# First feed-forward's output projection as seven block products, its weight sums on GpSimd, and 12 modulation tiles moved behind the convolution

## The reference, cut to what matters

```
mod_x = split(silu(c) @ w_ada + b_ada, 9)          # 9 x 1024 modulation values, and mod_c from c_ctx
def ffn_half(s, shift, scale, gate, g_pre, g_post, w_in, w_out):
    h = (silu(gate_part) * up_part) @ w_out         # gate_part, up_part = split(modulate(rmsnorm(s, g_pre)) @ w_in)
    return s + 0.5 * gate * rmsnorm(h, g_post)
xs = ffn_half(xs, ...)                              # 256 tokens, D_FF = 2816, D_MODEL = 1024
cs = ffn_half(cs, ...)                              # 256 context tokens, the same weights
hx = modulate(rmsnorm(xs, g[2]), mod_x[3], mod_x[4])
hc = modulate(rmsnorm(cs, g[2]), mod_c[3], mod_c[4])
z_hy, q, k, v, gates = split(hx @ w_in)             # z_hy: 3 x 1024 columns, then a 3-tap convolution over tokens
```

## Time and profile before

| | us |
|---|---|
| median of 3 runs | 1926.42 (1924.99 to 1927.2) |
| the profiled execution's own time | 1927.17 |
| its span | 1925.4 |
| TensorE busy | 1732.5 (90%) |
| VectorE busy | 874.4 (45%) |
| ScalarE busy | 308.7 (16%) |
| GpSimd busy | 164.6 (9%) |

### The profile page before, as it was taken

The page is one execution under the profiler, slowest core; times in us unless marked ns, Lnnn a source line. Parts: engine busy times, 40 slices in busy tenths (PEclk is TensorE's granted clock), DMA queues, the critical chain, the costliest instruction groups (busy, mean ns, idle before and its releaser), DMA issues.

```text
span 1925.4 us, 28951 instructions
## 1 busy us (share of the span) xinstructions
PE 1732.5 (90%) x11848; PEld 1371.0 (71%) x11848; DVE 874.4 (45%) x1760; ACT 308.7 (16%) x697; POOL 164.6 (9%) x159
## 2 busy tenths in 40 slices
PE   8999999999999999999999999999999765655656
PEld 3888888888888989679999998877778221221214
DVE  5766666965466466644676136743433000000001
ACT  2200000010210002422111114322323000000001
POOL 3000000010133310001000002612001000000000
PEclk9999999999999999999999999989999987787878
DMA  9433334965442214126545863101379999999997
GB/s 374 148 130 129 128 130 160 346 244 197 153 153 88 88 45 154 66 87 220 195 171 179 291 213 130 45 24 46 131 279 377 407 430 433 430 432 433 430 432 302
DMA packets 47043, 426.04 MB, mean 221 GB/s; under 512 B 5364, under 2 KB 5973, under 8 KB 16093
## 3 DMA queue, kind: packets, MB, share of 16 engines
q1 hardware_dynamic: 37296, 386.97, 51.7%
q10 hardware_dynamic: 9644, 37.59, 5.4%
HBM read 423.49 MB, written 1.05 MB: 220 GB/s over the span
## 4 chain that ended last, share of the span: by engine, by line
PE 71%; DMA 18%; DVE 5%; issue 2%; ACT 2%; POOL 1%; POOLq 0%; SPq 0%; ACTq 0%; DVEq 0%
PE bank L1027 26%; DMA arena<-experts_ring_dram 18%; PE bank L1161 13%; PE bank L1211 8%; PE bank L1595 3%; PE bank L1310 3%; PE bank L1308 3%; PE bank L1664 2%; PE bank L1969 2%; PE bank L1488 1%; ACT arena L2254 1%; DVE arena L3232 1%; DVE tiny L3034 1%; PE bank L1363 1%; PE bank L1353 1%
## 5 line engine op out<-in xcount | busy, mean ns | idle before, releaser
L1027 PE MATMUL bank<-arena 128*128 128x256 f32 (+1 forms) x2912 | 507.5, 336 | 0.5 <-ACT arena L2471 0.5
L1027 PEld LDWEIGHTS bank<-arena 128*128 128x128 f32 x2912 | 459.2, 191 | 46.6 <-issue 1.8
L1969 PE MATMUL bank<-arena 128*32 128x512 f32 x1400 | 213.2, 763 | 145.3 <-DMA arena<-experts_ring_dram 145.3
L1969 PEld LDWEIGHTS bank<-arena 128*32 128x32 f32 x1400 | 58.1, 135 | 293.5 <-issue 293.3
L1161 PE MATMUL bank<-arena 128*128 128x256 f32 x880 | 193.9, 379 | 0.0
L1161 PEld LDWEIGHTS bank<-arena 128*128 128x128 f32 x880 | 167.1, 190 | 23.1 <-issue 0.5
L1211 PE MATMUL bank<-arena 128*128 128x128 f32 x1456 | 162.9, 275 | 0.0
L1211 PEld LDWEIGHTS bank<-arena 128*128 128x128 f32 x1456 | 162.8, 192 | 0.1
L3426 DVE TENSOR_TENSOR arena<-arena,bank 128x512 f32<-128x512 f32 x8 | 5.5, 688 | 240.8 <-PE bank L1969 240.8
L905 POOL TENSOR_TENSOR rstd<-sq 128x128 f32<-128x128 f32 (+2 forms) x9 | 6.7, 740 | 971.6 <-ACT sq L2091 971.6
L2732 DVE SCALAR_TENSOR_TENSOR arena<-arena 128x1024 f32<-128x1024 f32 x56 | 68.3, 1221 | 0.0
(11 more groups left out here) (500 smaller groups left out, 2233.8 us busy)
## 6 DMA issues: line engine op xcount, KB each, us to landing
arena<-dense_dram SPq DMA_DIRECT2D x167, 1024.0 KB, 4.9
arena<-experts_ring_dram SPq DMA_DIRECT2D x41, 4096.0 KB, 26.9
arena<-ada_rest_dram ACTq DMA_DIRECT2D x56, 512.0 KB, 5.5
arena<-experts_dram SPq DMA_DIRECT2D x18, 1024.0 KB, 8.8
arena<-ada_head_dram SPq DMA_DIRECT2D x8, 1024.0 KB, 23.6
arena<-experts_dram SPq DMA_DIRECT2D x10, 512.0 KB, 9.4
arena<-tokens_dram ACTq DMA_DIRECT2D x1, 2048.0 KB, 20.7
arena<-experts_ring_dram SPq DMA_DIRECT2D x1, 2048.0 KB, 23.5
```

Source lines behind the costliest of these rows:

```text
L1027: ins = mm(out, lhsT=w, rhs=rhs(k), start=k == 0, stop=k == k_tiles - 1)
L1969: ins = mm(ps[banks[half]][32 * e:32 * e + 32, :], lhsT=lhs[:, 2 * kp + par, CAP * e:CAP * e + CAP], rhs=slab[e][par][:, half * 512:half * ...
```

## The change

`ffn1_out` is computed as seven block products too. A pair of output tiles (2p, 2p+1) is one step p of 4, for r=0 and then r=1. The 22 hidden blocks split into two halves of 11, and the 11 go in three slabs c of 4, 4 and 3 blocks in each half; seven 128-column accumulation regions in two banks (0,1 for even p, 2,3 for odd p) stay open over the three slabs. That makes 24 slabs of which every third is only three quarters full, where there were 22.

- TensorE: `out_products`, 7 x 4 (or 7 x 3) matmuls of 128 columns in each slab.
- GpSimd: for each of the 24 slabs four tensor_tensors of 128 x 512 (128 x 384 for the third slab), after it has waited for all of `hid1`; `sum_squares(2)` stands behind slab 17.
- VectorE: four token sums for each c and r (24 tensor_tensors of SBUF data, 128 x 512 or 128 x 384), five joins for each (r, p) out of the banks, and 16 ada tiles instead of 28 in r=0, in groups of four ahead of the join of each p; 8 in r=1 as before, in two groups; the other 12 stand in the loop over `z`, one after each of tiles 2 to 13.
- ScalarE: one 128 x 128 copy for each (r, p), and the squares are taken from SBUF after the join. Its 8 last ada loads stand in the `z` loop.
- The context's norm (`stat_of_sum(3)`, `inverse_root(3)`) and its residual start one tile of `z` later.

```diff
-ADA_FIRST, ADA_SECOND = 28, 8
+ADA_FIRST, ADA_SECOND = 16, 8
+OUT_HALF, OUT_STEPS = FT // 2, 3
+OUT_SUMMED = KD * OUT_STEPS
@@ GpSimd
-            sum_squares(2, T)
+            pool.wait_ge(in_hid, FT)
+            for n in range(OUT_SUMMED):
+                slab, s, made, nk = SLAB0["ffn1_out"] + n, n % 2, 4 * FT + 4 * n, len(out_step(n % OUT_STEPS))
...
+                pool.wait_ge(slab_loaded[slab % RING], 16 * (slab // RING + 1))
+                if n > 1:
+                    pool.wait_ge(ws_used, FT + n - 1)
+                nc.gpsimd.tensor_tensor(s1, w2, w3, add).then_inc(ws_ready, 1)
+                pool.wait_ge(ws_ready, made + 1)
+                nc.gpsimd.tensor_tensor(s2, s1, w0, sub).then_inc(ws_ready, 1)
+                nc.gpsimd.tensor_tensor(w2, w0, w2, sub).then_inc(ws_ready, 1)
+                pool.wait_ge(ws_ready, made + 2)
+                nc.gpsimd.tensor_tensor(s4, w1, s2, sub).then_inc(ws_ready, 1)
+                if n == OUT_SUMMED // 2 + 5:
+                    sum_squares(2, T)
@@ TensorE
+            def out_products(r, p, c):
...
+                out_region(a, 0, w0, first_a, nk, first, False, slab_started)
+                out_region(a, P, w1, first_b, nk, False, False)
+                pe.wait_ge(ot_ready, 12 * r + 4 * c + 2)
+                pe.wait_ge(ws_ready, 4 * FT + 4 * n + 2)
+                out_region(a, 2 * P, s2, t2, nk, False, False)
+                ins = out_region(a, 3 * P, s1, t1, nk, False, last)
...
+                pe.wait_ge(ot_ready, 12 * r + 4 * c + 4)
+                pe.wait_ge(ws_ready, 4 * FT + 4 * n + 4)
+                out_region(b, 0, s4, second_b, nk, first, False)
+                out_region(b, P, w2, t3, nk, False, False)
+                ins = out_region(b, 2 * P, w3, t4, nk, False, last, ws_used)
...
-            for t in range(2 * KD):
-                take(pe, "ffn1_out", t % 4, t // 4)
-                product(ps[t % 4][:, 0:T], FT, lambda k: x_then_ctx(t, k), full[t % 4],
-                        arrived=None if t else last_hidden(in_hid))
-                first_norms(t)
+            for r in range(2):
+                for p in range(KD // 2):
+                    for c in range(OUT_STEPS):
+                        out_products(r, p, c)
+                        if (r, p, c) == (1, 0, 1):
+                            stat_of_sum(1, T)
+                        elif (r, p, c) == (1, 2, 1):
+                            stat_of_sum(2, T)
@@ VectorE
+            def out_token_sums(r, c):
+                a1, a2, b1, b2 = out_hidden(r, c)
+                t1, t2, t3, t4 = out_tokens(r, c)
+                tt_(t1, a2, a1, sub).then_inc(ot_ready, 1)
...
+                tt_(t2, b2, t1, sub).then_inc(ot_ready, 1)
+                tt_(t3, b2, a2, sub).then_inc(ot_ready, 1)
...
+                tt_(t4, b1, t2, sub).then_inc(ot_ready, 1)
...
+            for p in range(KD // 2):
+                for n in range(ADA_FIRST // 4 * p, ADA_FIRST // 4 * p + ADA_FIRST // 4):
+                    ada_late(n, y1[:, 0:4, T:2 * T])
+                if p:
+                    out_sums(0, p - 1)
+                out_join_first(0, p)
+                if p == KD // 2 - 1:
+                    got(dve, "ffn1_out", 3, 1)
+                    out_token_sums(1, 0)
+                out_join_second(0, p)
+            for c_ in range(1, OUT_STEPS):
+                out_token_sums(1, c_)
+            out_sums(0, KD // 2 - 1)
...
+            out_join_first(1, 0)
+            out_join_second(1, 0)
+            for p in range(2):
+                for n in range(ADA_SECOND // 2):
+                    ada_late(ADA_FIRST + ADA_SECOND // 2 * p + n, page(7, D).rearrange("p (k n) -> p k n", n=T))
+                if p == 0:
+                    out_sums(1, 0)
+                    out_join_first(1, 1)
+                    out_join_second(1, 1)
...
+            for p in range(2, 4):
+                out_sums(1, p - 1)
+                out_join_first(1, p)
+                out_join_second(1, p)
+            out_sums(1, 3)
@@ VectorE, the loop over z
-                if 1 <= n <= KD + 1:
-                    ctx_residual(n - 1)
+                if 2 <= n <= KD + 2:
+                    ctx_residual(n - 2)
...
+                if 2 <= n < 2 + ADA_TILES - ADA_IN - ADA_FIRST - ADA_SECOND:
+                    ada_late(ADA_FIRST + ADA_SECOND + n - 2, fh)
```

More of the change, by code:

```diff
@@ L253, in slabs, with out_slabs @@
     return b.reshape(-1, 16, P, P).transpose(0, 2, 1, 3).reshape(-1, P, SLAB)
+def out_slabs(w):
+    b = blocks(w)
+    out = np.zeros((KD // 2, OUT_STEPS, 16, P, P), b.dtype)
+    for p in range(KD // 2):
+        for c in range(OUT_STEPS):
+            ks = list(out_step(c))
+            for n, (o, lo) in enumerate(((0, 0), (0, OUT_HALF), (1, 0), (1, OUT_HALF))):
+                out[p, c, n * len(ks):n * len(ks) + len(ks)] = b[2 * p + o][[lo + k for k in ks]]
+    return slabs(out)
 def wide(w, n=256):
@@ L299, in lay_out @@
     dense = np.concatenate([
-        slabs(f1), *(slabs(blocks(g["w_ff_out"][0, 0])) for _ in range(2)), slabs(blocks(w_in[:, :5 * D])),
+        slabs(f1), *(out_slabs(g["w_ff_out"][0, 0]) for _ in range(2)), slabs(blocks(w_in[:, :5 * D])),
         wide(w_in[:, 5 * D:6 * D]), slabs(first_gates[:2 * GATE_PAIRS]),
@@ L623, in build @@
         in_hid = sem("in_hid")
+        ot_ready = sem("ot_ready")
         tt_ready = sem("tt_ready")
@@ L930, in _ @@
             for n in range(8):
-                slab, s, made = SLAB0["k"] + n, n % 2, 4 * FT + 4 * n
+                slab, s, made = SLAB0["k"] + n, n % 2, 4 * (FT + OUT_SUMMED) + 4 * n
                 w0, w1, w2, w3 = kv_blocks(n)
@@ L1267, in ctx_norms, with out_region @@
                     stat_of_sum(4, T)
+            def out_region(b, o, lhs, rhs, n, start, stop, started=None):
+                for k in range(n):
+                    ins = mm(ps[b][:, o:o + P], lhsT=lhs[:, k, :], rhs=rhs[:, k, :], start=start and k == 0, stop=stop and k == n - 1)
+                    if k == 0 and started is not None:
+                        ins.then_inc(started, 1)
+                return ins
+            def out_products(r, p, c):
+                n, nk, (a, b), use = 12 * r + 3 * p + c, len(out_step(c)), TWO_SETS[p % 2], 2 * r + p // 2
+                s, first, last = n % 2, c == 0, c == OUT_STEPS - 1
+                slot = st.slab % RING
+                assert st.slab == SLAB0["ffn1_out"] + n
+                w0, w1, w2, w3 = (ring[slot][:, m * nk:m * nk + nk, :] for m in range(4))
+                s1, s2, s4 = (v_[s] for v_ in (out_s1, out_s2, out_s4))
+                first_a, _, first_b, second_b = out_hidden(r, c)
+                t1, t2, t3, t4 = out_tokens(r, c)
+                pe.wait_ge(slab_loaded[slot], 16 * (st.slab // RING + 1))
+                st.slab += 1
+                if r == p == 0:
+                    pe.wait_ge(in_hid, OUT_HALF + out_step(c)[-1] + 1)
+                if first:
+                    take(pe, "ffn1_out", a, use)
+                out_region(a, 0, w0, first_a, nk, first, False, slab_started)
[4 more added lines that the diff above has]
+                ins = out_region(a, 3 * P, s1, t1, nk, False, last)
+                if last:
+                    ins.then_inc(full[a], 1)
+                if first:
+                    take(pe, "ffn1_out", b, use)
+                pe.wait_ge(ot_ready, 12 * r + 4 * c + 4)
[3 more added lines that the diff above has]
+                ins = out_region(b, 2 * P, w3, t4, nk, False, last, ws_used)
+                if last:
+                    ins.then_inc(full[b], 1)
             def last_hidden(made):
@@ L2195, in _ @@
                 square(2, j, X[:, j, 0:T], T)
[L2196 to L2203, removed]
+            for p in range(KD // 2):
+                if p == 2:
+                    root(2, T)
+                out_copy(1, p)
+                out_squares(1, p)
+                if p < 2:
+                    for n in range(ADA_SECOND // 2):
+                        ada_late_load(ADA_FIRST + ADA_SECOND // 2 * p + n)
             for n in range(24):
```

118 lines of the change are left out of this document (84 added, 34 removed).

## The result

The changed kernel takes 1962.31 us (median of 4 runs, 1960.02 to 1962.5) against 1926.14 for the kernel before in the same comparison: ratio 1.0185 [1.0168, 1.0203], slower by 36 us. The forecast was 1978 us, with a range of 1940 to 2002. The profiled execution took 1962.5 us with a span of 1960.6, so its rows explain the measured time.

The account below looks back on a forecast made before the run. The prediction took TensorE (90% of the span) as the bound before the change. It summed 1927.2 + 42 (stage) + 6 (z) + 4 (clock) = 1979, given as 1978 us against the median of the runs, range 1940 to 2002.

Parts of the forecast that it names:

- rival 2: `ffn1_out`: turns are taken but orders interlock better, port hardly rests; stage +30, z +3, clock 0: 1960 us; chance 23%.
- TensorE's gain, -16.7: `ffn1_out`: 1232 records of 128 columns take 137.9 us in place of 154.6; alone -16.7 us.
- Turns, 2.22 us each: `ffn1_out`: VectorE's ada operations and GpSimd's 512-wide sums alternate at the SBUF port, 1.27 + 1.22 - 0.27 = 2.22 us.
- The port budget as floor, 181: `ffn1_out`: GpSimd and VectorE two-SBUF-input work, less turn savings, needs at least 181 us against 154.6 before.
- The turn to r=1: Slab 12: TensorE waits from 414 to 430 us for VectorE's token sums, queued behind the join of step 3.
- The norm's wait, 440.8 to 444.7: First norm in r=1: TensorE waits 440.8 to 444.7 us behind VectorE's eight token sums and two square sums.
- The end: End of `ffn1_out`: slab 18's s2 at 470.5, TensorE done about 514, z starts at 519.3 us; stage +42.
- z, +6: z: VectorE falls 11 us behind, banks allow 10.6; waits for residual, reciprocal and squares cost +6 us (bounds 0 and 14).
- Clock, +4: `ffn1_out`: TensorE's granted clock drops after long waits, partly hidden by following waits; +4 us (bounds 0 and 20).
- Rival 1: `ffn1_out`: ada operations don't collide with GpSimd, TensorE stays the bound: 1919.6 us, faster; chance 13%.
- Rival 3: `ffn1_out` and z: 1.2 GHz clock after each long wait, +20 instead of +4, z lateness at upper bound: 2000 us; 11%.
- Rival 4: `ffn1_out`: 128-column products keep starving and miss 0.112 us, other waits just balance: within 0.2%; chance 3%.

Follow-up runs that it names:

- e2: Changed kernel with GpSimd's weight sums cut to 32 columns and TensorE multiplying the slab's own blocks in their place: 1917.23 us, ratio 0.9949.
- e1b: Changed kernel with the stage's 24 ada tiles reading their second input from a bank, in four 512-column operations a tile: 1925.79 us, ratio 0.9989.
- e6: Changed kernel with 40 ada tiles in `ffn1_in` (two a step), none in the stage, 16 in z: 1930.66 us, ratio 1.0022.
- e11: e9 with slab 0's weight sums made during the last slab of `ffn1_in`, in that stage's buffers: 1923.39 us, ratio 0.998.
- e9: e6 with four ada tiles moved from z to r=0 and r=1's first token sums ahead of the last join: 1923.8 us, ratio 0.9985.
- e4: Changed kernel with no ada tile in z: 28 in r=0, 8 in r=1: 1997.93 us, ratio 1.0364.

## Why the prediction was right, and where its numbers were not

The mechanism was right in its core and in most of its steps; the size was 16 us too high. The time lies in the stated range but not in the 1966 to 1992 to which the forecast itself gave 50%; it lies where rival 2 was. Luck has a part in the sum: the stage was priced too high and the clock too low. By the steps of the prediction:

- **TensorE's gain, -16.7.** Measured -14.7 without waits (153.0 to 138.3 in e2). The products came at 0.112 us as worked out. Mis-sized was the term before: z began at 475.4 us, not 477.0, so the old stage was 153.0 us and its records 0.217 apart. The last stretch that I had cut reached into z.
- **Turns, 2.22 us each.** Right: starts 2.21 apart, means 1.91 and 2.21, 1.24 once the sums are short (e2).
- **The port budget as floor, 181.** The stage took 188.1: 7 us over the floor, where the timeline that I laid out had 197 (322.4 to 519.3). GpSimd or a VectorE operation on SBUF data alone was running in about 183 of the 188.1, so the port rests little.
- **The steps of r=0** were to end at 344.8, 368, 390 and 412. By the record count in TensorE's timeline they ended near 345.9, 369.2, 392.9 and 415.9, up to 4 us later than worked out; 0.9 of it was there at the start (last hidden block at 324.74 in place of 323.83).
- **The turn to r=1.** VectorE was to come to the join at 427, and came at 421.9; slab 12 was to go on at 430 and did at 425.4. The wait is there, for the reason given, but 7.6 us long in place of 16: 5 us of the error.
- **The norm's wait, 440.8 to 444.7.** It didn't occur: the statistic's product ran at 438.8 and no wait is recorded there. TensorE got slab 18's `s2` (L969) 5.9 us earlier than forecast (464.65 against 470.5), still after a wait (1.55 us, for GpSimd).
- **The end.** z at 510.5 against 519.3 forecast, 8.8 us earlier. 5.9 of them were there at slab 18. Steps 2 and 3 of r=1 then took what was worked out: from that `s2` to TensorE's last product 43.6 us against 43.5. The other 3 us are the wait in front of z: VectorE began to normalise at 501.2 in place of 508.5, and from 505 us on had the port to itself, so z waited 2.2 us for the join in place of 5.3.
- **z, +6.** Measured +0.45. VectorE does fall behind, and ScalarE does wait for it, up to 2.8 us, but TensorE never. Mis-sized was the lateness: the taps of tile 14, the latest, start at 571.85, 7.6 us later than ScalarE's scaling of that tile would let them (563.67 + 0.56), where 11 were worked out, and the banks' 10.6 weren't reached. It cost time only with 16 tiles (116.3, +2.9) and with 20 (128.8, +15.4).
- **Clock, +4.** It fell where a long wait stood (0.58 behind the turn, 2.7 us there; 0.93 over the stage). The lower level came after waits of 2.4 us as well, so the products lost 11.2 us to it where +4 was taken. How much of that the kernel paid cannot be taken out of the 35.1 us, because most slow slabs are followed by a wait.
- **Together.** The forecast put +42, +6 and +4. The stage with its clock measured +35.1 and z +0.45: a sum of +35.6 in place of +52. About 11 of the 16 us are the stage and its clock, the rest z. If the kernel paid all of the 11.2 us of clock, the stage without it cost +24; if none, +35. The +42 was too high either way.
- **The rivals.** Rival 1 (no collision) is refuted by the rows and by e2 and e1b, though e2 shows its world: 1917.2 against the 1919.6 worked out for it. Rival 2 (a better interlock, 1960) hit the time within 2.3 us and describes the stage best: the port hardly rests. Its terms were less exact than its sum: +30 for the stage was 5 too low, +3 for z 2.5 too high, and it took no clock. Rival 3's place for the clock was right, its price of +20 too high against those 11.2. Rival 4 has nothing for it.

Between e6's stage (150.7) and e2's (139.5) lie 11.2 us: 8.0 of more waits (9.15 idle against 1.2) and 3.2 of longer busy time, of which the clock of 0.99 can be half. What the rest of the 3.2 is stays open. Of the changed kernel's 16.2 us of longer busy time (154.56 against 138.32) the clock is 11.2; that the other 5 are products that start late inside a group of records is likely, but not shown. It was not tried to make the first token sums and the last hidden block earlier, which is what the start of e11 waits for.

## What to carry to other kernels

Before moving work to an idle engine, add up the times of all operations that would share its SBUF port in that stage; an engine at 0% with a neighbour at 89% is not free, and the sum, not each engine's own time, is what has to fit under the bound. Move the neighbour's movable work to where the other engine is empty (here 20 ada tiles went into `ffn1_in` at no measurable cost), or let it read from a bank (e1b, which is a test of the time alone: its modulations are wrong). What is left then are the starts of stages, where both kinds of sums begin at once and the bound engine waits for the first of them.

## What the runs showed of the hardware that was not expected

A tiny operation pays a whole turn: the 128x8 bias addition on SBUF inputs took 1.06 us on average beside GpSimd (L2844, 6 of them) and 0.16 at 323.86, ahead of GpSimd's first sum, so a chain of small operations there would be dear. And short waits already lowered the granted clock: waits of 3.3 and 0.7 us at the start of the stage went with 0.77 over the 12.6 us around them (e9), and inside the gap of 15.6 us it was 0.50 for ten of them (e4), so that a wait costs more than its own length.
